# GpSimd takes the last expert of each group in the second joint attention stage of a hybrid mLSTM / attention / PEER layer

## The reference, cut to what matters

```python
act = jax.nn.gelu(jnp.einsum('thkd,td->thk', u_tab[idx], xb), approximate=False)
out = jnp.einsum('thk,thkd->td', (g * act), v_tab[idx])      # h += out
```

## Time and profile before

| | us |
|---|---|
| median of 3 runs | 5003.93 (4996.28 to 5006.18) |
| the profiled execution, its own time | 5006.99 |
| its span in the profile | 5005.3 |
| VectorE busy over the span | 3075.7 (61%) |
| TensorE busy (matmul) | 4349.9 (87%) |
| GpSimd busy | 1255.3 (25%) |

### The profile page before, as it was taken

The page is one execution under the profiler, slowest core; times in us unless marked ns, Lnnn a source line. Parts: engine busy times, 40 slices in busy tenths (PEclk is TensorE's granted clock), DMA queues, the critical chain, the costliest instruction groups (busy, mean ns, idle before and its releaser), DMA issues. The chain is left out here.

```text
span 5005.3 us, 48598 instructions
## 1 busy us (share of the span) xinstructions
PE 4349.9 (87%) x16974; PEld 2671.5 (53%) x16974; DVE 3075.7 (61%) x6269; ACT 953.0 (19%) x1784; POOL 1255.3 (25%) x970
## 2 busy tenths in 40 slices
PE   8996687849999986888887889467999999999988
PEld 5555454635555555666664656454554445444534
DVE  1002340577666657888870566887777777777742
ACT  1113221101001104555541111131000000000023
POOL 0000030004444442333320000001444444444410
PEclk9998788969999997787778999799999999999999
DMA  4433588629999988987858777167999999999941
GB/s 169 148 131 100 185 275 324 246 107 421 389 378 391 385 336 277 333 301 288 313 199 329 266 274 270 70 225 273 418 418 419 419 414 415 414 416 410 414 193 56
DMA packets 338726, 1477.72 MB, mean 295 GB/s; under 512 B 38146, under 2 KB 153650, under 8 KB 217938
## 3 DMA queue, kind: packets, MB, share of 16 engines
q0 software_dynamic: 119872, 824.76, 41.0%
q1 hardware_dynamic: 218642, 650.30, 35.0%
HBM read 1369.00 MB, written 115.38 MB: 297 GB/s over the span
## 5 line engine op out<-in xcount | busy, mean ns | idle before, releaser
L2286 POOL DMA_INDIRECT ex_uv<-in_uv,idx x768 | 1164.5, 1516 | 1936.5 <-DVE ex_acc L2343 1688.1
L2327 DVE CUSTOM_DVE_ANT_0 ex_uv<-ex_uv,ex_xp 128x1024 f32<-128x1024 f32 x768 | 913.5, 1221 | 312.5 <-DMA ex_uv<-in_uv,idx 274.9
L2343 DVE SCALAR_TENSOR_TENSOR ex_acc<-ex_uv,ex_wt,ex_acc 128x1024 f32<-128x1024 f32 x768 | 942.9, 1281 | 11.1 <-DVE C L880 3.6
L384 PE MATMUL proj_psum_acc<-proj_w,aT_later 128*128 128x385 f32 x2304 | 749.9, 487 | 62.4 <-DMA proj_w<-in_w_in 62.4
L2633 PE MATMUL exp_psum_dn<-exp_dn_big,exp_dn_gg 128*128 128x512 f32 x1536 | 686.6, 597 | 26.4 <-DVE exp_dn_gg L2555 26.4
L2624 PE MATMUL exp_psum_dn<-exp_dn_xT,exp_dn_big 128*128 128x384 f32 x2048 | 683.5, 487 | 14.4 <-DMA exp_dn_big<-in_ud 14.4
L384 PEld LDWEIGHTS proj_psum_acc<-proj_w,aT_later 128*128 128x128 f32 x2304 | 437.5, 190 | 374.3 <-DMA proj_w<-in_w_in 62.6
L2624 PEld LDWEIGHTS exp_psum_dn<-exp_dn_xT,exp_dn_big 128*128 128x128 f32 x2048 | 390.2, 191 | 314.2 <-issue 61.9
L2633 PEld LDWEIGHTS exp_psum_dn<-exp_dn_big,exp_dn_gg 128*128 128x128 f32 x1536 | 291.8, 191 | 376.9 <-issue 349.3
L296 PE MATMUL proj_psum_acc<-proj_w,aT 128*128 128x385 f32 x1152 | 377.0, 488 | 3.6 <-DVE aT L230 1.9
L1955 PE MATMUL rt_psum_b<-rt_w,rt_yT 128*128 128x512 f32 x576 | 269.4, 631 | 50.0 <-ACT rt_yT L2021 42.4
(11 more groups left out here) (374 smaller groups left out, 4226.7 us busy)
## 6 DMA issues: line engine op xcount, KB each, us to landing
proj_w<-in_w_in SPq DMA_DIRECT2D x48, 1540.0 KB, 12.6
rt_w<-in_w_q SPq DMA_DIRECT2D x36, 2048.0 KB, 8.1
exp_dn_big<-in_ud SPq DMA_DIRECT2D x128, 512.0 KB
exp_dn_big<-in_vd SPq DMA_DIRECT2D x128, 512.0 KB
scratch_z<-proj_zs SPq DMA_DIRECT2D x216, 192.5 KB
rt_w<-in_w_br_m SPq DMA_DIRECT2D x18, 2048.0 KB, 9.9
rt_w<-in_w_br_f SPq DMA_DIRECT2D x18, 2048.0 KB
rt_w<-in_w_out SPq DMA_DIRECT2D x18, 2048.0 KB, 9.8
```

Of the source, the lines that this page charges most:

```text
L384: mm = pe.matmul(acc[j % SLOTS][:, 0:CW], aT[:, k, t * P:(t + 1) * P], w[:, u % U, k, :], start=(k == 0), stop=(k == KD - 1))
L2286: pool.indirect_dma_start(self.uv[:, slot, :], None, self.uv_tab, bass.IndirectOffsetOnAxis(ap=self.idx[:, at:at + 1], axis=0)).then_inc(s ...
L2327: dve.tensor_tensor_reduce(self.uv[:, slot, 0:D], self.uv[:, slot, 0:D], self.xp[:], 1.0, 0.0, ALU.mult, ALU.add, self.dot[:, g % 2, j:j + ...
L2343: dve.scalar_tensor_tensor(out=self.acc[:, j % 2, :], in0=self.uv[:, slot, D:2 * D], scalar=self.wt[:, g % 2, j:j + 1], in1=self.acc[:, j ...
```

## The change

`Experts` gets a group number `pool_from` from which on GpSimd helps; the joint object is given `EARLY` (52). A group is pooled where its number is at least 52 and it is not one of the first two groups of its tile: groups 52 to 63 and 66 to 95, 42 in all. In a pooled group VectorE accumulates experts 0, 1 and 2 only (alternating between its accumulators by a running count), and GpSimd the fourth, in two instructions: it multiplies the v row by its weight in place, and adds the product to `sum`, which serves as its accumulator and is set to zero by GpSimd before the first pooled group of a tile. `dve_end` then adds `sum` to the second accumulator before the two are joined. GpSimd does this ahead of the fetches of the same turn of its loop, so those are behind it in its queue. The projection stage (groups below 52) and `stage_experts` are as before.

```diff
     def fetch(self, pool, g):
...
-            if g >= 2:
-                pool.wait_ge(self.added, (g - 2) * G + j + 1)
+            if g >= 2 and j == G - 1 and self.pooled(g - 2):
+                pool.wait_ge(self.pool_added, self.pool_adds(g - 1))
+            elif g >= 2:
+                pool.wait_ge(self.added, self.adds(g - 2) + j + 1)
...
     def pool_span(self, pool, g0, g1):
         self.pool_ahead(pool, g0)
         for g in range(g0, g1):
+            if self.pooled(g):
+                self.pool_add(pool, g)
             if g + self.AHEAD < self.GROUPS:
                 self.fetch(pool, g + self.AHEAD)
+
+    def pool_add(self, pool, g):
+        t, r = divmod(g, self.PER_TILE)
+        n, j = self.pool_adds(g), self.G - 1
+        slot = g % 2 * self.G + j
+        if n == self.pool_adds(t * self.PER_TILE):
+            if t >= 1:
+                pool.wait_ge(self.stored, t * 16)
+            pool.memset(self.sum[:], 0.0).then_inc(self.pool_zeroed, 1)
+            pool.wait_ge(self.pool_zeroed, sum(self.pool_shares(u) for u in range(t + 1)))
+        pool.wait_ge(self.weighed, g + 1)
+        pool.wait_ge(self.uv_in[slot], (g // 2 + 1) * 16)
+        if n >= 1:
+            pool.wait_ge(self.pool_added, n)
+        v = self.uv[:, slot, D:2 * D]
+        pool.tensor_scalar(v, v, self.wt[:, g % 2, j:j + 1], None, ALU.mult).then_inc(self.pool_scaled, 1)
+        pool.wait_ge(self.pool_scaled, n + 1)
+        pool.tensor_tensor(self.sum[:], self.sum[:], v, ALU.add).then_inc(self.pool_added, 1)
...
     def dve_end(self, dve, t):
-        dve.wait_ge(self.added, (t + 1) * EXPERTS)
-        if t >= 1:
+        dve.wait_ge(self.added, self.adds((t + 1) * self.PER_TILE))
+        if self.pool_shares(t):
+            dve.wait_ge(self.pool_added, self.pool_adds((t + 1) * self.PER_TILE))
+            dve.tensor_tensor(self.acc[:, 1, :], self.acc[:, 1, :], self.sum[:], ALU.add).then_inc(self.halved, 1)
+            dve.wait_ge(self.halved, sum(self.pool_shares(u) for u in range(t + 1)))
+        elif t >= 1:
             dve.wait_ge(self.stored, t * 16)
         dve.tensor_tensor(self.sum[:], self.acc[:, 0, :], self.acc[:, 1, :], ALU.add).then_inc(self.joined, 1)
...
-        else:
+        elif unit < 2 * G or not self.pooled(g):
             j = unit - G - 1
+            n = self.adds(g) + j
...
-                ex = Experts(nc, K, rings, 0, HOSTED, idx, gate, A["uv"], T)
+                ex = Experts(nc, K, rings, 0, HOSTED, idx, gate, A["uv"], T, EARLY)
```

More of the change, by code:

```diff
@@ L2257, with __init__ @@
     UNITS = 2 * G + 1
-    def __init__(self, nc, K, ctx, tile0, nt, idx, gate, uv_tab, T, by_pool=False):
+    def __init__(self, nc, K, ctx, tile0, nt, idx, gate, uv_tab, T, pool_from=None):
         def sb(name, shape, dt=F32):
@@ L2268, in __init__ @@
         self.tile0, self.nt, self.GROUPS = tile0, nt, nt * self.PER_TILE
+        self.pool_from = self.GROUPS if pool_from is None else pool_from
         self.uv = sb("uv", [P, 2 * G, 2 * D])
@@ L2274, in __init__, with pooled, pool_adds, adds @@
         (self.dotted, self.added, self.geluted, self.weighed, self.xp_set, self.acc_set, self.zeroed, self.joined,
-         self.x_in, self.h_in, self.stored) = (
+         self.x_in, self.h_in, self.stored, self.pool_added, self.pool_zeroed, self.halved,
+         self.pool_scaled) = (
             sem(n) for n in ("dotted", "added", "geluted", "weighed", "xp_set", "acc_set", "zeroed", "joined",
-                             "x_in", "h_in", "stored"))
+                             "x_in", "h_in", "stored", "pool_added", "pool_zeroed", "halved", "pool_scaled"))
+    def pooled(self, g):
+        return g >= self.pool_from and g % self.PER_TILE >= 2
+    def pool_adds(self, g):
+        return sum(self.pooled(n) for n in range(g))
+    def adds(self, g):
+        return g * self.G - self.pool_adds(g)
+    def pool_shares(self, t):
+        return self.pool_adds((t + 1) * self.PER_TILE) > self.pool_adds(t * self.PER_TILE)
     def fetch(self, pool, g):
@@ L2331, in dve_unit @@
             if g >= 2:
-                dve.wait_ge(self.added, (g - 1) * G)
+                dve.wait_ge(self.added, self.adds(g - 1))
+                if self.pooled(g - 2):
+                    dve.wait_ge(self.pool_added, self.pool_adds(g - 1))
             at = (self.tile0 * self.PER_TILE + g) * G
@@ L2340, in dve_unit @@
                 dve.wait_ge(self.weighed, g + 1)
[L2341 to L2344, removed]
+            if n >= 2:
+                dve.wait_ge(self.added, n - 1)
+            dve.scalar_tensor_tensor(out=self.acc[:, n % 2, :], in0=self.uv[:, slot, D:2 * D],
+                                     scalar=self.wt[:, g % 2, j:j + 1], in1=self.acc[:, n % 2, :],
                                      op0=ALU.mult, op1=ALU.add).then_inc(self.added, 1)
```

## The result

| | before | after |
|---|---|---|
| median of 7 runs each, us | 4999.97 (4994.56 to 5011.96) | 5025.03 (5013.85 to 5030.27) |
| ratio of after to before | | 1.0046, 95% interval 1.0032 to 1.0060 |
| span of the profiled execution, us | 5005.3 | 5026.4 |

The changed kernel is 0.46% slower, about 23 us. I had forecast 33 us slower, between 22 us faster and 72 us slower.

The account below looks back on a forecast made before the run. VectorE was taken to bound the second attention stage. Removing 50 us, adding 80 of holding and 3 at tile ends gave +33 us: 5040 against the profiled execution, 5037 as median, range 4982 to 5076.

Parts of the forecast that it names:

- What bounds the stage: Second attention stage: VectorE, busy 598.5 of 690 us, is the longest part most of the time.
- the ring: Each attention step: maximum, exponential, scores, maximum; VectorE with hosted work between two maxima is its longest part mostly.
- Removed, 50 us: Second attention stage: 42 accumulations, 1.20 us apart, leave VectorE, 50 us.
- I let it through whole: The +33 us on VectorE was taken as the stage's full lengthening, none hidden in the 34.5 us waiting for scores.
- GpSimd's instructions: Added per pooled group: multiplication 1.11 us (0.95 reading) and addition 2.04 us (1.9 reading).
- VectorE held: VectorE instructions with two SBUF inputs wait for GpSimd's long reads: 1.9 us a group, 80 us over 42 groups.
- the walk: One group stepped through: multiplication delays add 1 by 0.2 us, addition delays add 2 by 2.0; costs 2.1, gains 1.2.
- Sum: VectorE in the second attention stage: -50 + 80 + 3 = +33 us.
- Ends of tiles, fetches, zeroing: Tile ending inside the stage: one more add and a wait for GpSimd, 3 us; fetches, zeroing and new waits nothing.
- Not held: Rival: GpSimd's reads don't hold VectorE, 30 us of the 50 gained, 4974 us; chance 0.18.
- cancelling: Rival: VectorE held only briefly (0.95 us each) or half on idle time, loss and gain cancel, 5002 us; chance 0.09.
- late fetches: Rival: GpSimd falls behind and experts come late, 42 x 2 us = 84, about 5090 us; chance 0.03.

Follow-up runs that it names:

- e3: Changed kernel, but VectorE accumulates all four experts as before and GpSimd does its multiplication and addition for nothing: 5053.99 us, ratio 1.0096 to before.
- e1: Changed kernel without GpSimd's multiplication and addition, so the pooled groups' fourth expert is missing: 4987.88 us, ratio 0.9972 to before.
- e6: As e1, with VectorE's units spread evenly over the halves of the steps: 4979.54 us, ratio 0.9947 to before.
- e2: Changed kernel with six zeroings of the v row in place of GpSimd's two instructions, fourth expert missing: 4997.92 us, ratio 0.9984 to before.
- e5: Changed kernel with GpSimd's addition only, no multiplication, so the fourth expert is added unweighted: 5041.63 us, ratio 1.0069 to before.
- e8: Changed kernel with GpSimd's addition cut into two halves, each waiting until VectorE comes to a row maximum: 5027.18 us, ratio 1.0046 to before.

## Why the prediction was right

- *What bounds the stage.* VectorE's part of the ring, right for loads added, half right for loads taken away. 68 us more on VectorE cost 49 (e3), 48 us less gave 16 (e1), 25 with the even spread (e6).
- *Removed, 50 us.* Right as VectorE's time (47.5, with 2.4 of joining adds against it). The step that failed is "I let it through whole": it is worth 16. The rows that spoke of it were those of the earlier trace rows: 34.5 us of waiting for scores and 36.6 for the gelu, and I priced it in the rival only (30 us).
- *GpSimd's instructions.* The addition was forecast at 2.04 us with 1.9 of reading and measured 2.34 with 2.15; the Trainium skill's figure (GPSIMD Engine Reference, Elementwise), 2.25 as an estimate, lay closer. The multiplication was forecast at 1.11 and is 2.85: the rate of the one-input selections of the earlier trace rows doesn't carry over to it. Its reading, forecast at 0.95, is 0.91.
- *VectorE held.* The step that decides was right in its mechanism, and was only faintly shown before. Forecast 80 us on VectorE; measured 66.9 (648.8 in the change against 581.9 in e1), of which accumulations 34.0, dots 12.9, and small steps of attention with two SBUF inputs most of the rest. Of these, the stage pays 37.6 us (783.9 to 746.3). In the walk, the addition came too early by 1.7 us and met the third accumulation; in the changed kernel it often meets the next group's dots, or attention's steps.
- *Sum.* +33 forecast as -50 + 80 + 3; measured +23, in the stage +21.7 as -15.9 and +37.6. Both terms were too large, in opposite directions and by 34 and 42 us, so much of the agreement is luck.
- *Ends of tiles, fetches, zeroing.* 1.0 us of waiting for the ring, and 2.4 us for the two joining adds with no wait for GpSimd before them: right. The slack of the fetches was not large: in e2, with 6.0 us of zeroing a group and a shorter stage, 8.1 us went to late experts.
- *Rivals.* "Not held" fell with the accumulations' 1534 ns in the change, "cancelling" with the addition's 2.34 us and with e5, late fetches with the 1.0 us above.

## What to carry to other kernels

Before giving GpSimd elementwise work beside a busy VectorE, count how many of VectorE's instructions have two SBUF inputs, and add the time for which GpSimd holds them, here 2.15 us for two inputs of 1024 columns and 0.91 for one, to VectorE's queue unless steps on PSUM cover it; an accumulation of 1.28 us was replaced by 1.6 us of holding. The sign is in a trace without any such work: GpSimd's issues take 0.94 us, or the rest of the running VectorE instruction plus 0.82. And price relief and load apart: in this ring of three engines 48 us less on VectorE gave 16, and 68 us more cost 49.

## What was not expected of the hardware

- GpSimd's multiplication by a scalar takes 2.85 us for 128x1024, longer than its addition of two tiles (2.34), and holds VectorE for the first 0.91 us only. The Trainium skill (SBUF — State Buffer, SBUF: two separate sides) has a contending VectorE instruction fully blocked while GpSimd's holds the pair for its whole instruction; here it ran beside the last 1.9 us. For the addition (held for 2.15 of 2.35 us) the rule agrees to 0.2 us.
- GpSimd's writing held other steps of VectorE than its reading. In e2, beside zeroings, dots and accumulations were untouched (1221, 1279 ns), while a scaling of 128x256 from SBUF to SBUF took 477 instead of 376 ns on average (e1) and a copy of 128x4 604 instead of 171.
- A count-up in VectorE's queue was carried out before the instructions ahead of it had ended: in e8 GpSimd was released by it at 2085.06, 0.7 us before the running dot's end and with another dot still to come. So it is no mark of where VectorE's data path stands.
